# Two-block transformer layer in fp32, one core: how attention probabilities are normalised and turned

## Chip, cores and metric

The kernel runs on one NeuronCore of a Trainium2 chip. Everything is fp32. The metric is the device time of one execution in microseconds (us).

## What is computed

Two blocks in a row on 256 tokens of width 1024. The first block is an adaptive-norm layer with a mixer of two attentions and a mixture of 32 experts; the second has a gated linear recurrence, an LRU and a dense feed-forward part. The change touches only the softmax of the two attentions of the first block. Both have 8 heads of width 64; one selects keys and adds a distance bias, the other adds a forgetting bias. What follows the logits is the same in both:

```python
    logits = jnp.where(causal[None, None], logits, -jnp.inf)
    p = jax.nn.softmax(logits, axis=-1).astype(v.dtype)
    o = jnp.einsum('bhqs,bshd->bqhd', p, v)
```

## The kernel before, in words

**Layout.** Activations lie transposed (features on partitions, `L` = 256 tokens in the free dimension). All weights pass through `ring`, four slots filled by SyncE's DMA queue. The eight PSUM banks are `ps[:, 0..7, :]`. Each engine has one program written out by hand, and semaphores tie them.

**Attention.** The 16 heads go in 8 pairs, p = 0 to 7 (0 to 3 the forgetting heads, 4 to 7 the selecting ones), two "halves" per pair. Queries lie on partitions in two blocks of 128: block 0 sees keys 0 to 127 (columns 0 to 127 of `logit` and `prob`), block 1 sees all 256 keys (columns 128 to 383), so that a half is 128 x 384. For each pair:

1. TensorE, `logits_of(p)` (L821, L826): the dot products, into banks 2 and 3.
2. VectorE, `logits(p)` (L1860 to L1874): bias and mask into `logit`, then the negated row maximum.
3. ScalarE, `softmax(p)` (L1470, L1472): exp into `prob`, row sums into `p_sum`. From pair 1 on it waits until the same half of the pair before has been turned (`pt_done`), as `prob` has one buffer per half.
4. VectorE, `diagonals(p)` (L1882, L1887): reciprocal of the sums, and for each of the two query blocks `diag` = identity times that reciprocal, 128 x 128.
5. TensorE, `turn_probs(p)` (L837): for each half three products `prob_block.T @ diag`, which turn a 128 x 128 block and scale it at once, into bank 4 or 5. It waits for `diag_ready`, and for `pt_taken` of the pair before.
6. ScalarE, `turned_probs(p)` (L1481): copies the bank to `probT`.
7. TensorE, `values(p)` (L849), and ScalarE, `mixed(p)` (L1487, L1488): the head outputs.

**What lies between.** On TensorE the steps of a pair are spread among other work. For pairs 0 to 4 the order is `turn_probs(p)`, `logits_of(p+1)`, a 16-record group of `features` (L730, input projection), `values(p)`, `ada_rows` (L689, the modulation rows), another `features`, `ada_cols` (L700), `turn_probs(p+1)`. Pair 5 has `features` around it; pairs 6 and 7 have pieces of the output projection, `out_b` (L919), around them. Then come `out_a` (L929) mixed with `route_part` (L977, L979 and plain transposes of `hT` on L985), the routing chain on VectorE, the gather product (L1017), the experts (L1028, L1036 and L1039 transposes, L1049, L1056), and the second block.

**VectorE between the pairs.** After `diagonals(p)` it waits for `ada_cols`, adds a bias (L1794) and does four k-tiles of the modulation product (`ada_steps`, L1765, L1768); only then comes `logits(p+1)`. After pair 5 it makes a reciprocal (L1906) and scales four tiles (L1909).

**DMA.** SyncE issues each load when an event of TensorE has freed its slot: modulation and input weights (L434, L440, L444) and the first four experts (L485, L490) during attention and output projection, and from the expert loop on, gate/up and down weights by pairs of experts, first at 250.1 us.

Of the kernel before, what the change touches and what calls it, by code (L numbers as in the profile page):

```python
# [23 lines left out]
ALU = mybir.AluOpType  # L24
# [4 lines left out]
P = 128  # L29
L = 256  # L30
BLK = L // P
# [97 lines left out]
def build(nc, x, c, w_ada, b_ada, g_mix, w_in, b_forget, g_out_a, g_out_b, w_out, g_ffn, w_group,  # L129
# [3 lines left out]
    with ExitStack() as ctx:  # L133
        def sb(name, shape, dt=F32):
            return ctx.enter_context(nc.sbuf_tensor(name, shape, dt))

        def sem(name):
            return ctx.enter_context(nc.semaphore(name))
# [8 lines left out]
        ident = sb("ident", [P, P])  # L147
# [14 lines left out]
        def cut(at, *shape):  # L162

            n = 1
            for s in shape:
                n *= s
            v = arena[:, at:at + n]
            if len(shape) == 2:
                v = v.rearrange("p (a b) -> p a b", b=shape[1])
            if len(shape) == 3:  # L170
                v = v.rearrange("p (a b c) -> p a b c", b=shape[1], c=shape[2])
            return v
# [20 lines left out]
        logit = cut(8192, 2, NK)  # L193
        prob = cut(8960, 2, NK)
        probT = cut(9728, 2, NK)
        diag = cut(10496, 2, BLK, P)
        causal = cut(11008, L)
        neg_dist = cut(11264, NK)
        head_row = cut(11648, HEADS, P)
# [8 lines left out]
        p_rsum = att_small[:, 80:112].rearrange("p (n b) -> p n b", b=BLK)  # L208
# [63 lines left out]
        def state(ch):  # L272

            return tokf[:, (ch - 1) * 512:ch * 512] if ch <= 4 else sqf[:, (ch - 5) * 512:(ch - 4) * 512]
# [51 lines left out]
        ps = ctx.enter_context(nc.psum_tensor("ps", [P, 8, 512], F32))  # L326
# [26 lines left out]
        forget_abs, forget_ln, log_f_ready = sem("forget_abs"), sem("forget_ln"), sem("log_f_ready")  # L353
        cum_done, cum_taken = sem("cum_done"), sem("cum_taken")
        logits_done, logits_taken, logits_ready = sem("logits_done"), sem("logits_taken"), sem("logits_ready")
        probs_ready, diag_ready = sem("probs_ready"), sem("diag_ready")
        pt_done, pt_taken, pv_done, pv_taken = sem("pt_done"), sem("pt_taken"), sem("pv_done"), sem("pv_taken")
        mix_ready = sem("mix_ready")
        mo_done, mo_taken = sem("mo_done"), sem("mo_taken")
# [252 lines left out]
        def _(pe):  # L612
# [19 lines left out]
            for q in range(4):  # L632
                for k in (2 * q, 2 * q + 1):
                    for b in range(BLK):
                        at = (k % 2) * L + b * P
                        last = pe.transpose(ps[:, q, at:at + P], tok[:, b, k * P:(k + 1) * P], ident[:])
# [33 lines left out]
            for i in range(8):  # L670
                last = pe.matmul(ps[:, 0, i:16:8], lhsT=row0[:, i // 4, (i % 4) * P:(i % 4 + 1) * P], rhs=both_halves,
                                 start=True, stop=True)
# [92 lines left out]
            for b in range(BLK):  # L765
                last = pe.transpose(ps[:, 6, 8 * b:8 * b + 8], kI[64:72, b * P:(b + 1) * P], ident[64:72, 64:72])
# [29 lines left out]
            for q in (slice(0, HEADS), slice(64, 64 + HEADS)):  # L796
                pe.matmul(ps[q, 6, 128:384], lhsT=lf[:, 0, :], rhs=tri[:], start=True, stop=False)
                last = pe.matmul(ps[q, 6, 256:384], lhsT=lf[:, 1, :], rhs=tri[:, 0:P], start=False, stop=True)
# [31 lines left out]
            def turn_probs(p):  # L830

                for half in range(2):
                    pe.wait_ge(diag_ready, 2 * p + half + 1)
                    if p:
                        pe.wait_ge(pt_taken, 2 * p - 1 + half)
                    for s in range(3):
                        last = pe.matmul(ps[:, 4 + half, s * P:(s + 1) * P], lhsT=prob[:, half, s * P:(s + 1) * P],  # L837
                                         rhs=diag[:, half, min(s, 1), :], start=True, stop=True)
                    last.then_inc(pt_done, 1)

            def values(p):
# [17 lines left out]
            features(2, P)  # L859
            ada_cols(1)  # L860
            turn_probs(0)
            pe.wait_ge(tile_taken, 13)
            logits_of(1)
# [37 lines left out]
            for k in range(4, KT):  # L901
                last = pe.matmul(ps[:, 7, 0:L], lhsT=ones[:], rhs=sq[:, k, :], start=k == 4, stop=k == KT - 1)
# [64 lines left out]
            for k in range(4):  # L967
                pe.wait_ge(pv_taken, 2 * k + 10)
                last = pe.matmul(ps[:, 7, 0:L], lhsT=ones[:], rhs=sq[:, k, :], start=k == 0, stop=k == 3)
# [30 lines left out]
            for b in range(BLK):  # L1000
                last = pe.transpose(ps[:, 5, b * 65:b * 65 + 65], raw_rows[0:65, b * P:(b + 1) * P], ident[0:65, 0:65])
# [10 lines left out]
            for b in range(BLK):  # L1012
                pe.wait_ge(pick_ready, b + 1)
                for j in range(KT):
                    if j == KT - 1:
                        pe.wait_ge(pick_ready, BLK)
                    last = pe.matmul(ps[:, j, :], lhsT=tok[:, b, j * P:(j + 1) * P], rhs=pick[:, b, :],  # L1017
                                     start=b == 0, stop=b == BLK - 1)
# [90 lines left out]
            with pe.Else():  # L1109
                clear_banks()  # L1110
                with pe.Fori(0, EXPERTS // SLOTS) as i:
                    for u in range(2):
                        e0 = 2 * u
                        with pe.Fori(0, WINDOWS) as w:
                            n = i * (2 * WINDOWS) + w + u * WINDOWS
# [38 lines left out]
            for i in range(4):  # L1154
                o = bank2()
                for k in range(KT):
                    if i == 0:
                        pe.wait_ge(raw_ready, k + 1)
                    last = pe.matmul(o[:, 0:L], lhsT=w[:, k, i * P:(i + 1) * P], rhs=h_raw[:, k, :], start=k == 0,  # L1159
                                     stop=k == KT - 1)  # L1160
# [19 lines left out]
            for g in range(2):  # L1180
                for j in range(4):
                    last = pe.matmul(ps[:, 4 + 2 * g + j // 2, (j % 2) * L:(j % 2 + 1) * L],
                                     lhsT=gate_w[:, g, j, :], rhs=xc[:, j, :], start=True, stop=True)
# [12 lines left out]
            for b in range(BLK):  # L1196
                for h in range(HG):
                    last = pe.transpose(ps[:, 4 + b, h * P:(h + 1) * P], ks[:, h, b * P:(b + 1) * P], ident[:])
# [3 lines left out]
            for b in range(BLK):  # L1202
                t = slice(b * P, (b + 1) * P)
                for h in range(HG):
                    last = pe.matmul(ps[:, 6 + b, h * P:(h + 1) * P], lhsT=kd[:, h, t], rhs=raw_q[:, h, t],
                                     start=True, stop=True)
# [31 lines left out]
            for h in range(HG):  # L1238
                n = slice(h * P, (h + 1) * P)
                o = ps[:, 4 + h // 2, (h % 2) * L:(h % 2 + 1) * L]  # L1240
                for b in range(BLK):
                    pe.matmul(o[:, b * P:(b + 1) * P], lhsT=v_[:, b, n], rhs=sc_[:, b, h, :],
                              start=h % 2 == 0 and b == 0, stop=False, skip_group_check=True)
                for ch in range(1, CHUNKS):
                    t = slice(ch * CHUNK, (ch + 1) * CHUNK)
                    last = pe.matmul(o[:, t], lhsT=state(ch)[:, n], rhs=raw_q[:, h, t], start=False,
                                     stop=ch == CHUNKS - 1, skip_group_check=True)
# [22 lines left out]
            for t in range(FT):  # L1270
                ch, i = divmod(t, FFN_STEP)
                n = min(FFN_STEP, FT - ch * FFN_STEP)
# [7 lines left out]
                for half in range(2):  # L1280
                    at = (half * n + i) * P
                    for k in range(KT):
                        if t == 0 and half == 0:
                            pe.wait_ge(scaled[4], k + 1)
                        last = pe.matmul(ps[:, t % 4, half * L:(half + 1) * L], lhsT=w[:, k, at:at + P],  # L1285
                                         rhs=hT[:, k, :], start=k == 0, stop=k == KT - 1)
# [11 lines left out]
            def down_product(t, j, last=False):  # L1298

                ch, i = divmod(t, DOWN_STEP)  # L1300
                w = weights("down", ch, min(DOWN_STEP, FT - ch * DOWN_STEP), D)
                return pe.matmul(ps[:, 4 + j // 2, (j % 2) * L:(j % 2 + 1) * L], lhsT=w[:, i, j * P:(j + 1) * P],  # L1302
                                 rhs=ffn[:, t, :], start=t == 0 and j % 2 == 0, stop=t == FT - 1, skip_group_check=True)
# [13 lines left out]
            for t in range(first_late):  # L1317
# [3 lines left out]
                for j in range(KT):  # L1321
                    last = down_product(t, j)
# [4 lines left out]
            for i in range(4):  # L1327
                for t in range(first_late, FT):
                    for j in (2 * i, 2 * i + 1):
                        last = down_product(t, j)  # L1330
# [372 lines left out]
        def _(ve):  # L1703
            step = Count()

            def own(k=1):

                ve.wait_ge(dve_step, step.up(k))
# [50 lines left out]
            def ada_steps(c):  # L1759

                w, part = weights("ada", c, KT, ada_width(c)), ada_part(c)
                ve.wait_ge(arrived[SLOT["ada", c]], ARRIVED["ada", c])
                if c >= 2:
                    ve.wait_ge(ada_rows_done, c)
                ve.tensor_scalar(part, w[:, 0, :], silu_c[:, 0:1], None, ALU.mult).then_inc(dve_step, 1)  # L1765
                for k in range(1, DVE_K):
                    own()
                    ve.scalar_tensor_tensor(part, w[:, k, :], silu_c[:, k:k + 1], part, ALU.mult, ALU.add  # L1768
                                            ).then_inc(ada_part_ready if k == DVE_K - 1 else dve_step, 1)
# [33 lines left out]
            keys = (slice(0, P), slice(P, NK))  # L1803
# [70 lines left out]
                        ve.tensor_reduce(neg_max[:, n, b:b + 1], logit[:, half, keys[b]], AX.X, ALU.max, negate=True  # L1874
                                         ).then_inc(logits_ready, 1)

            def diagonals(p):

                for half in range(2):
                    n = 2 * p + half  # L1880
                    ve.wait_ge(probs_ready, n + 1)
                    ve.reciprocal(p_rsum[:, n, :], p_sum[:, n, :]).then_inc(dve_step, 1)  # L1882
                    own()
                    if p:
                        ve.wait_ge(pt_done, n - 1)
                    for b in range(BLK):
                        i = ve.tensor_scalar(diag[:, half, b, :], ident[:], p_rsum[:, n, b:b + 1], None, ALU.mult)  # L1887
                    i.then_inc(diag_ready, 1)

            for p in range(5):  # L1890
                logits(p)
                diagonals(p)
                add_bias(p + 1) if p < 4 else None
                if p < 4:
                    ada_steps(p + 2)
# [5 lines left out]
                             ).then_inc(dve_step, 1)  # L1901
            own(2)
            logits(5)
            diagonals(5)
            ve.wait_ge(std_ready, STD["b"])
            ve.reciprocal(rstd[:, 1, :], rstd[:, 1, :]).then_inc(dve_step, 1)  # L1906
            own()
# [1 line left out]
                ve.scalar_tensor_tensor(mixT[:, k, :], mixT[:, k, :], parB[:, k:k + 1], rstd[:, 1, :],  # L1909
                                        ALU.mult, ALU.mult).then_inc(mix_ready, 1)  # L1910
            logits(6)
            diagonals(6)
            logits(7)
            diagonals(7)


            lb0, lb1, lru = par(parB, PB_ROWS, "lb0"), par(parB, PB_ROWS, "lb1"), par(parB, PB_ROWS, "lru_a")
# [186 lines left out]
            with ve.Else():  # L2104
                with ve.Fori(0, EXPERTS // 2) as i:
                    with ve.Fori(0, WINDOWS) as w:
                        n = i * WINDOWS + w
# [118 lines left out]
            for ch in range(CHUNKS - 1):  # L2226
# [5 lines left out]
                for h in range(HG):  # L2232
                    n = slice(h * P, (h + 1) * P)
                    last = ch * CHUNK + CHUNK - 1
                    i = ve.scalar_tensor_tensor(state(ch + 1)[:, n], state(ch)[:, n], eb[:, h, last:last + 1],
                                                ps[:, 4 + ch % 4, n], ALU.mult, ALU.add)
# [86 lines left out]
```

## Time and profile before

| what | value |
|---|---|
| median of 3 runs | 872.6 us (872.42, 872.6, 874.89) |
| the profiled execution | 875.01 us |
| its span, first to last instruction | 873.3 us |
| mean granted TensorE clock | 0.985 |
| attention with its turns | about 86 to 190 us |
| output projection and routing | 190 to 224 us |
| gather and experts | 224 to 480 us |
| second block | 480 to 873 us |

How to read it: PE is TensorE's matmuls, PEld its weight loads, DVE VectorE, ACT ScalarE, SPq SyncE's DMA queue. An fp32 product of the program appears as two records (L837 has 96 for 48 products), a transpose as one (L985 has 16 for 16). A record's duration reaches past the start of the next, so that the rate is read from distances between starts, not from durations.

### The profile page before, as it was taken

Reading aid. Unit: us, or ns where it says so; the run is one execution under the profiler, and the core shown is the slowest. Engines: PE = TensorE matmul, PEld = TensorE weight load, DVE = VectorE, ACT = ScalarE, POOL = GpSimd, SP = SyncE. Lnnn points to the kernel's source line nnn. Section 1 sums busy time; section 2 is a strip of 40 time slices with the busy share of each in tenths; the row PEclk is TensorE's granted clock in tenths of the full one; section 3 lists DMA queues with packets and bytes.
Section 4 is the critical chain, followed back from the end, with each engine's and each line's share of the span. In section 5 each row is a group of like instructions: output and inputs, shape, how many; then the busy total and the mean of one; then the engine's idle time right before and its main releaser. Section 6 shows DMA issues by size and latency. Waiting matters only on the chain.

```text
span 873.3 us, 10154 instructions
## 1 busy us (share of the span) xinstructions
PE 829.3 (95%) x4067; PEld 592.2 (68%) x4067; DVE 264.5 (30%) x650; ACT 171.7 (20%) x360; POOL 14.4 (2%) x37
## 2 busy tenths in 40 slices
PE   4999999998789999999999889999999999999997
PEld 3578777786335454444444776788888888888886
DVE  4138546554412121212111576344111111110003
ACT  4123323433301010101101328122210000000001
POOL 2100000000010000000000000000000000000000
PEclk9999999999799999999999999998999999999999
DMA  9988665426159999999999922224434442444001
GB/s 374 374 230 302 235 247 199 167 123 244 46 211 418 418 417 420 414 420 416 419 417 318 338 97 97 70 77 143 152 137 145 145 144 53 160 168 199 0 1 49
DMA packets 67037, 196.58 MB, mean 225 GB/s; under 512 B 2767, under 2 KB 30776, under 8 KB 57784
## 3 DMA queue, kind: packets, MB, share of 16 engines
q1 hardware_dynamic: 66192, 195.37, 58.9%
q0 software_dynamic: 288, 0.41, 0.2%
q8 instruction: 27, 0.44, 0.2%
q10 hardware_dynamic: 520, 0.28, 0.1%
q14 instruction: 10, 0.08, 0.0%
HBM read 194.80 MB, written 1.05 MB: 224 GB/s over the span
## 4 chain that ended last, share of the span: by engine, by line
PE 83%; DMA 11%; DVE 2%; ACT 1%; issue 1%; SPq 0%; DVEq 0%
PE ps L1285 17%; DMA ring<-in_w_down 10%; PE ps L1302 9%; PE ps L1028 8%; PE ps L626 8%; PE ps L730 7%; PE ps L1049 4%; PE ps L1056 4%; PE ps L957 3%; PE ps L739 2%; PE ps L689 2%; PE ps L1017 2%; PE ps L919 2%; PE ps L929 2%; PE ps L1159 1%; PE ps L837 1%
## 5 line engine op out<-in xcount | busy, mean ns | idle before, releaser
L1285 PE MATMUL ps<-hT,ring 128*128 128x256 f32 x704 | 152.3, 379 | 0.9 <-DVE xT L2264 0.9
L1285 PEld LDWEIGHTS ps<-hT,ring 128*128 128x128 f32 x704 | 133.7, 190 | 19.4 <-issue 1.3
L1028 PE MATMUL ps<-ring,arena 128*64 128x512 f32 x512 | 113.2, 594 | 5.4 <-DMA ring<-in_w_down 3.1
L1028 PEld LDWEIGHTS ps<-ring,arena 128*64 128x64 f32 x512 | 38.8, 137 | 79.0 <-issue 73.0
L1302 PE MATMUL ps<-arena,ring 128*128 128x256 f32 x352 | 76.7, 380 | 0.3 <-PE ps L1285 0.3
L1302 PEld LDWEIGHTS ps<-arena,ring 128*128 128x128 f32 x352 | 66.6, 190 | 9.6 <-issue 0.7
L730 PE MATMUL ps<-hT,ring 128*128 128x256 f32 (+1 forms) x288 | 67.5, 390 | 1.2 <-ACT hT L1397 1.2
L730 PEld LDWEIGHTS ps<-hT,ring 128*128 128x128 f32 (+1 forms) x288 | 53.5, 190 | 13.9 <-issue 6.2
L1056 PE MATMUL ps<-arena 128*128 128x256 f32 x256 | 62.0, 386 | 0.9 <-DVE arena L2074 0.9
L1049 PE MATMUL ps<-ring,arena 128*64 128x512 f32 x256 | 58.5, 599 | 0.7 <-ACT arena L1575 0.7
L1056 PEld LDWEIGHTS ps<-arena 128*128 128x128 f32 x256 | 46.1, 190 | 18.9 <-issue 12.2
L626 PE MATMUL ps<-hT,ring 128*128 128x256 f32 x256 | 56.6, 380 | 2.4 <-DVE arena L2144 2.1
L626 PEld LDWEIGHTS ps<-hT,ring 128*128 128x128 f32 x256 | 48.2, 190 | 9.7 <-DVE hT L2139 2.5
L2275 DVE TENSOR_TENSOR arena<-ps,rstd 128x256 f32<-128x256 f32 x22 | 9.3, 424 | 120.4 <-PE ps L1285 120.3
L2071 DVE TENSOR_TENSOR arena<-arena,ps 128x256 f32<-128x256 f32 x16 | 6.7, 421 | 113.5 <-ACT arena L1573 113.5
L1049 PEld LDWEIGHTS ps<-ring,arena 128*64 128x64 f32 x256 | 17.0, 136 | 33.3 <-issue 32.4
L1687 ACT ACTIVATE arena<-arena 128x256 f32<-128x256 f32 x22 | 9.2, 416 | 135.1 <-DVE arena L2275 135.1
L2074 DVE COPY arena<-ps 128x512 f32<-128x512 f32 x16 | 11.1, 692 | 81.0 <-PE ps L1049 81.0
L957 PE MATMUL ps<-mixT,ring 128*128 128x256 f32 x128 | 28.6, 383 | 0.1
L957 PEld LDWEIGHTS ps<-mixT,ring 128*128 128x128 f32 x128 | 24.7, 193 | 5.3 <-issue 2.0
L1573 ACT ACTIVATE arena<-ps 128x256 f32<-128x256 f32 x16 | 6.2, 384 | 110.6 <-PE ps L1028 110.6
L2286 DVE TENSOR_TENSOR xT<-ps,xT 128x512 f32<-128x512 f32 x4 | 2.8, 691 | 73.6 <-PE ps L1302 73.6
(381 smaller groups left out, 848.4 us busy)
## 6 DMA issues: line engine op xcount, KB each, us to landing
ring<-in_w_gate SPq DMA_DIRECT2D x32, 1024.0 KB, 10.2
ring<-in_w_up SPq DMA_DIRECT2D x32, 1024.0 KB, 12.2
ring<-in_w_down SPq DMA_DIRECT2D x32, 1024.0 KB, 12.7
ring<-in_w_gate_up SPq DMA_DIRECT2D x14, 1536.0 KB, 9.4
ring<-in_w_ada SPq DMA_DIRECT2D x5, 3072.0 KB, 11.9
ring<-in_w_ada SPq DMA_DIRECT2D x9, 1024.0 KB, 13.0
ring<-in_w_in SPq DMA_DIRECT2D x9, 1024.0 KB, 15.8
ring<-in_w_down SPq DMA_DIRECT2D x3, 3072.0 KB, 10.2
```

What stands on the lines that cost most here:

```text
L626: last = pe.matmul(o, lhsT=w_of(k), rhs=rhs_of(k), start=k == 0, stop=k == k_n - 1)
L689: last = pe.matmul(ps[64 * half:64 * half + 64, 7, 0:n], lhsT=silu_b[:, k, :] if k < KT else ones[:, 0:64], rhs=w[:, k, cols] if k < KT el ...
L730: last = pe.matmul(o[0:n, 0:L], lhsT=w[:, k, lo:lo + n], rhs=hT[:, k, :], start=k == 0, stop=k == KT - 1)
L739: last = pe.matmul(o[:, i * n:(i + 1) * n], lhsT=hT[:, k, b * P:(b + 1) * P], rhs=w[:, k, lo:lo + n], start=k == 0, stop=k == KT - 1 and f ...
L919: last = pe.matmul(ps[:, m // 2, (m % 2) * L:(m % 2 + 1) * L], lhsT=w[:, k, (m % 4) * P:(m % 4 + 1) * P], rhs=mixT[:, k, :], start=m % 2 = ...
L929: last = pe.matmul(ps[:, 4 + m // 2, (m % 2) * L:(m % 2 + 1) * L], lhsT=w[:, k, (m % 4) * P:(m % 4 + 1) * P], rhs=mixT[:, k, :], start=m % ...
L957: last = pe.matmul(o, lhsT=w[:, k, (m % 4) * P:(m % 4 + 1) * P], rhs=mixT[:, k, :], start=last_of is None and m % 2 == 0 and k % 4 == 0, s ...
L1028: last = pe.matmul(ps[WIN * h:WIN * (h + 1), 0, :].rearrange("p (g n) -> p g n", g=2), lhsT=xw[:, u, k, WIN * h:WIN * (h + 1)], rhs=gu_w[: ...
L1049: last = pe.matmul(ps[WIN * h:WIN * (h + 1), 2 + half, :], lhsT=turned[:, u, at:at + WIN], rhs=dn[:, k, half * 512:(half + 1) * 512], star ...
L1056: last = pe.matmul(ps[:, 4 + j // 2, (j % 2) * L:(j % 2 + 1) * L], lhsT=y_sb[:, j * P:(j + 1) * P], rhs=turned[:, u, FE:FE + L], start=Fal ...
L1285: last = pe.matmul(ps[:, t % 4, half * L:(half + 1) * L], lhsT=w[:, k, at:at + P], rhs=hT[:, k, :], start=k == 0, stop=k == KT - 1)
L1302: return pe.matmul(ps[:, 4 + j // 2, (j % 2) * L:(j % 2 + 1) * L], lhsT=w[:, i, j * P:(j + 1) * P], rhs=ffn[:, t, :], start=t == 0 and j % ...
```

## The change

Instead of scaling an identity matrix and multiplying by it, VectorE scales `prob` in place, 128 columns for query block 0 and 256 for block 1, and TensorE turns each 128 x 128 block with its transpose against the constant identity. The tile `diag` goes, the semaphore is renamed, and VectorE's wait on `pt_done` ahead of writing `diag` goes.

```diff
@@ turn_probs (TensorE)
                 for half in range(2):
-                    pe.wait_ge(diag_ready, 2 * p + half + 1)
+                    pe.wait_ge(scaled_probs, 2 * p + half + 1)
                     if p:
                         pe.wait_ge(pt_taken, 2 * p - 1 + half)
                     for s in range(3):
-                        last = pe.matmul(ps[:, 4 + half, s * P:(s + 1) * P], lhsT=prob[:, half, s * P:(s + 1) * P],
-                                         rhs=diag[:, half, min(s, 1), :], start=True, stop=True)
+                        last = pe.transpose(ps[:, 4 + half, s * P:(s + 1) * P], prob[:, half, s * P:(s + 1) * P], ident[:])
                     last.then_inc(pt_done, 1)
@@ VectorE
-            def diagonals(p):
+            def scale_probs(p):
 
                 for half in range(2):
                     n = 2 * p + half
                     ve.wait_ge(probs_ready, n + 1)
                     ve.reciprocal(p_rsum[:, n, :], p_sum[:, n, :]).then_inc(dve_step, 1)
                     own()
-                    if p:
-                        ve.wait_ge(pt_done, n - 1)
                     for b in range(BLK):
-                        i = ve.tensor_scalar(diag[:, half, b, :], ident[:], p_rsum[:, n, b:b + 1], None, ALU.mult)
-                    i.then_inc(diag_ready, 1)
+                        i = ve.tensor_scalar(prob[:, half, keys[b]], prob[:, half, keys[b]], p_rsum[:, n, b:b + 1], None,
+                                             ALU.mult)
+                    i.then_inc(scaled_probs, 1)
```

All eight calls of `diagonals(p)` become `scale_probs(p)` at the same places.

## Rows read from the trace of the kernel before

**Rows 1.** The page: busy time by engine, and the chain that ended last.

```profile
PE 829.3 (95%) x4067; PEld 592.2 (68%) x4067; DVE 264.5 (30%) x650; ACT 171.7 (20%) x360; POOL 14.4 (2%) x37
...
PE 83%; DMA 11%; DVE 2%; ACT 1%; issue 1%; SPq 0%; DVEq 0%
```

**Rows 2.** Busy time by stretch: us, PE, PEld, DVE, ACT, POOL busy, clock, DMA share, GB/s.

```profile
98.00:190.00 92.00, 90.91 (x606) 71.96 (x605) 50.99 (x147) 34.71 (x107) 0.00 (x0) 1.00 0.59 224
190.00:220.00 30.00, 25.02 (x135) 19.52 (x133) 12.80 (x42) 11.20 (x20) 0.74 (x4) 0.97 0.55 201
```

**Rows 3.** Chain of waits in order of time: start us, us, what; the turns' pieces.

```profile
98.78 1.44 PE ps L837 x12
...
159.25 0.57 DVE arena L1860
...
165.50 0.39 ACT arena L1409
...
183.29 1.54 PE ps L837 x12
...
202.38 0.59 PE ps L985 x4
```

**Rows 4.** PE's timeline, two windows on pair 0's turn: start us, us, what.

```profile
98.64 1.58 PE L837 MATMUL ps<-arena 128*128 128x128 f32 x12
...
99.06 1.06 PE L837 MATMUL ps<-arena 128*128 128x128 f32 x8
```

**Rows 5.** PE's timeline, two windows on one group of transposes of `hT`.

```profile
202.31 0.66 PE L985 MATMUL ps<-ident,hT 128*128 128x128 f32 x4
...
202.48 0.49 PE L985 MATMUL ps<-ident,hT 128*128 128x128 f32 x3
```

**Rows 6.** Groups by line and shape, DVE, 84 to 190 us: busy us, mean ns.

```profile
L1887 DVE TENSOR_SCALAR arena<-ident,arena 128x128 f32<-128x128 f32 x32 | 7.7, 283 | 0.6
...
L1909 DVE SCALAR_TENSOR_TENSOR mixT<-mixT,parB,rstd 128x256 f32<-128x256 f32 x4 | 1.7, 481 | 0.0
...
L1765 DVE TENSOR_SCALAR tok<-ring,silu_c 128x256 f32<-128x256 f32 x1 | 0.4, 352 | 0.0
```

**Rows 7.** Timelines of DVE, ACT and PE around the turns of pairs 1, 5, 6, 7.

```profile
106.67 0.48 DVE L1887 TENSOR_SCALAR arena<-ident,arena 128x128 f32<-128x128 f32 x2
...
113.49 1.58 PE L837 MATMUL ps<-arena 128*128 128x128 f32 x12
...
164.14 0.48 DVE L1887 TENSOR_SCALAR arena<-ident,arena 128x128 f32<-128x128 f32 x2
...
166.79 1.60 PE L837 MATMUL ps<-arena 128*128 128x128 f32 x12
...
175.68 0.48 DVE L1887 TENSOR_SCALAR arena<-ident,arena 128x128 f32<-128x128 f32 x2
...
177.54 1.50 PE L837 MATMUL ps<-arena 128*128 128x128 f32 x12
...
180.63 0.84 ACT L1481 ACTIVATE arena<-ps 128x384 f32<-128x384 f32 x2
...
180.96 0.48 DVE L1887 TENSOR_SCALAR arena<-ident,arena 128x128 f32<-128x128 f32 x2
...
182.42 0.87 PE L849 MATMUL ps<-arena 128*64 128x256 f32 x8
...
183.22 1.60 PE L837 MATMUL ps<-arena 128*128 128x128 f32 x12
```

**Rows 8.** SyncE's queue, first expert loads of the loop; chain at the DMA-bound stage.

```profile
250.14 0.35 SPq L485 DMA_DIRECT2D ring<-in_w_gate x1
...
300.06 14.07 DMA ring<-in_w_down
```

**Rows 9.** Busy time by stretch, a fall of the clock and the 4 us behind it.

```profile
488.00:492.00 4.00, 4.00 (x12) 3.21 (x12) 3.82 (x7) 0.77 (x1) 0.00 (x0) 0.57 1.08 354
492.00:496.00 4.00, 4.00 (x21) 3.51 (x20) 0.83 (x2) 0.00 (x0) 0.00 (x0) 1.00 1.09 362
```

**Rows 10.** Single lines: transposes early and late in the trace, duration ns min/median/max.

```profile
L646 PE MATMUL ps<-ident,mixT x16: 421/421/448, 16.2 to 19.4; 128*128 128x128 f32 x16
...
L985 PE MATMUL ps<-ident,hT x16: 272/273/332, 202.3 to 215.7; 128*128 128x128 f32 x16
```

More of the change, by code:

```diff
@@ L195, in build @@
         probT = cut(9728, 2, NK)
-        diag = cut(10496, 2, BLK, P)
         causal = cut(11008, L)
@@ L355, in build @@
         logits_done, logits_taken, logits_ready = sem("logits_done"), sem("logits_taken"), sem("logits_ready")
-        probs_ready, diag_ready = sem("probs_ready"), sem("diag_ready")
+        probs_ready, scaled_probs = sem("probs_ready"), sem("scaled_probs")
         pt_done, pt_taken, pv_done, pv_taken = sem("pt_done"), sem("pt_taken"), sem("pv_done"), sem("pv_taken")
@@ L1883, in diagonals @@
                     own()
-                    if p:
-                        ve.wait_ge(pt_done, n - 1)
                     for b in range(BLK):
-                        i = ve.tensor_scalar(diag[:, half, b, :], ident[:], p_rsum[:, n, b:b + 1], None, ALU.mult)
-                    i.then_inc(diag_ready, 1)
+                        i = ve.tensor_scalar(prob[:, half, keys[b]], prob[:, half, keys[b]], p_rsum[:, n, b:b + 1], None,
+                                             ALU.mult)
+                    i.then_inc(scaled_probs, 1)
             for p in range(5):
                 logits(p)
-                diagonals(p)
+                scale_probs(p)
                 add_bias(p + 1) if p < 4 else None
@@ L1903, in _ @@
             logits(5)
-            diagonals(5)
+            scale_probs(5)
             ve.wait_ge(std_ready, STD["b"])
@@ L1911, in _ @@
             logits(6)
-            diagonals(6)
+            scale_probs(6)
             logits(7)
-            diagonals(7)
+            scale_probs(7)
             lb0, lb1, lru = par(parB, PB_ROWS, "lb0"), par(parB, PB_ROWS, "lb1"), par(parB, PB_ROWS, "lru_a")
```

## The prediction

> **What bounds the kernel.** I began with the page: TensorE is busy 95% of the span and the chain that ended last runs over it for 83% [rows 1]. What counts is the stretch with the turns, so next the busy time by stretch: from 98 to 190 us TensorE is busy 90.9 of 92 us, at granted clock 1.00, while VectorE has 51.0 and ScalarE 34.7 [rows 2]. All eight turns are there. Then the chain in order of time: every turn lies on it as one TensorE piece, 1.44 us for pair 0 and 1.54 for pair 7 [rows 3], and the six between are 1.34 to 1.53, 11.8 us in sum. The only stretch between turns where TensorE is not the bound begins at the end of pair 5's logits, 159.2 us: VectorE and ScalarE carry the chain until ScalarE's copy at 165.5 us [rows 3]. It starts from a TensorE event, so that it moves with it. TensorE time taken out of a turn is thus time taken out of the chain, as long as nothing else is late.
>
> **TensorE, the term that counts.** Before, a turn is six products, 12 records. In the middle of a turn 8 records span 1.06 us, the last of them 0.275 long, so (1.06 - 0.275)/7 = 0.112 us lie between starts [rows 4]; a product is two records, 0.224 us. After, the turn is six transposes. The trace has the very operation, 128 x 128 fp32 against the identity, at full clock: three on L985 span 0.49 us with a last one of 0.273, so (0.49 - 0.273)/2 = 0.109 us lie between starts [rows 5, 10]. A transpose takes one record where a product takes two, at nearly the same spacing. 8 pairs x 6 = 48, and 48 x (0.224 - 0.109) = 5.5 us. That is the upper bound. For the lower bound I take whole pieces of the chain with their heads: four transposes on L985 are 0.59 us there, 0.148 each [rows 3], so six are 0.885 and eight turns 7.1 us against 11.8: 4.7 us. Part of those 0.59 us is the first distance (0.17 us from 202.31 to 202.48 [rows 5]), paid once per group, and a turn has such a head before as well: it runs 1.58 us from 98.64, where 11 even distances and a last record would be 1.51 [rows 4]. I am therefore near the upper end and take 5.4 us.
>
> A rule that speaks against this. The L985 records are 273 ns long [rows 10], yet start 0.109 us apart. The Trainium skill, "TensorE: Matmul & The Clock Gate", Part 4 (PE-mode transpose), gives about 275 ns for a 128x128 transpose inside a kernel. The trace agrees as to a record's length and not as to the rate; read as a cost paid one after another, the page's figure would make 48 x 0.275 = 13.2 us of the turns, 1.4 us more than now.
>
> **VectorE.** Per half, two 128-column multiplications (0.48 us as a pair [rows 7], 283 ns each [rows 6]) become one of 128 and one of 256 columns. A 256-column tensor_scalar from and to SBUF takes 352 ns [rows 6]: 0.07 us more per half, 1.1 us in all. In place is not shown for this form; the nearest row is L1909, which writes where it reads with a third operand, 481 ns [rows 6]. That is the upper bound: 0.2 us per half, 3.2 in all; the lower is 0. I take 0.07, as the form with one tensor operand is the nearer. It costs nothing as long as the scaled half is there when TensorE asks:
> - Pairs 0 to 4: VectorE finishes pair 1 at 107.15 us and the turn starts at 113.49 [rows 7]; 6.3 us of cover. The other four of this form stand alike.
> - Pair 5: done at 164.62, turned at 166.79 [rows 7]. 2.2 us, fixed by the chain between, since both follow the same ScalarE copy or lie ahead of it.
> - Pair 6: done at 176.16, turned at 177.54 [rows 7]. 1.4 us; the second half alone decides, and it needs 0.07 to 0.2.
> - Pair 7: done at 181.44; turned at 183.22 [rows 7], now 0.7 us sooner, since pair 6's turn lies between. 1.1 us of cover, less twice 0.07.
>
> **What is late next.** `values(6)` at 182.42 us would come at 181.74. It needs ScalarE's two copies, which end at 181.47 [rows 7] and sit behind exp of pair 7, itself behind VectorE's maxima, themselves behind pair 6's scaling: 0.07 us later. 181.5 plus a semaphore step against 181.7: it just fits; with the slow in-place price it would wait some 0.1 us. I book 0.1 us in the 5.4. The exp of the next pair waits for the turn of the one before, which comes sooner. VectorE's dropped wait on `pt_done` is worth nothing: the exp it follows has waited for the same turn. `diag` takes no DMA; no queue, load or issue is moved.
>
> **Does the gain reach the end?** The loads of attention are released by TensorE events, and a pair's loop shrinks by 0.7 us at a time, with loads landing microseconds ahead (DMA share only 0.59 there [rows 2]). The experts are bound by DMA from 300 us (a piece of 14.07 us on the chain [rows 8]), but their loop's first issue, at 250.14 us [rows 8], is itself released by TensorE's work; the stream starts sooner by the same 5.4 us. So nothing swallows it.
>
> **Sum.** Against the profiled execution: 875.01 - 5.4 = 869.6 us, a span of 873.3 - 5.4 = 867.9. That execution was 2.4 us above the median of 872.6, one of the three runs (874.89) lies with it and two at 872.4 to 872.6. By the median: 872.6 - 5.4 = 867.2 us. No change that a measurement here can tell is within 0.3%, 2.6 us.
>
> **Rivals.**
> 1. *Half the gain is given back by the cover of the late pairs.* If a scaled half comes 1 us later than reckoned at pairs 6 and 7, TensorE waits there. Against it: 0.07 to 0.2 us are added where over 1 us is free. To matter each of four instructions must take 0.5 us more; then 1 to 2 us go, and the time is 868.2 to 869.2, still faster. If the turns also have only the lower bound's 4.7 us, 870 or just above: within 0.3%. 9%.
> 2. *The clock, ending slower.* Granted clock is 1.00 through all turns [rows 2]. Place: the 14 us periods with the turns. Were the clock to fall to its lower level once a turn, each fall would cost what the one at 488 us costs: 12 matmul records in 4 us, against 21 in the next 4 [rows 9], 9/21 x 4 = 1.7 us. Eight are 13.7 us: 872.6 - 5.4 + 13.7 = 880.9 us. It decides from the fourth fall on (3 x 1.7 = 5.1 is still paid by the gain; to be slower by over 0.3% takes five). For it: the transposes on L646 took 421 ns each where the later ones took 273 [rows 10], so 16 in a row from 16.2 to 19.4 us ran at the slow pace. Against it: those on L985 came in groups of four from 202 to 216 us at full pace, among products as here, and a turn is now only 0.7 us between dense products. 4%. The same page and part of the Trainium skill say that the clock gate does not count transposes as activity; by that rule the L646 row is as expected, and the turns would be 0.7 us holes, which this trace does not show to matter.
> 3. *It does not do what it says:* the turns' time is set by something other than the number of records, such as the stationary tile's load, and a transpose next to attention data costs as a product: no gain, 872.6. Against it: L985 has the same shape, types and roles, 0.109 apart [rows 5]. 3%.
> 4. *The clock's falls elsewhere move* as everything after 190 us comes sooner: the fall at 488 us and its like may be 1.7 us shorter or longer, and the runs' spread of 2.5 us is of this size. This shifts the result both ways and is in the range, not a case.
>
> My forecast, gain 4.7 to 5.5 us to the end, has 84%.
>
> **Range.** Low: 872.6 - 5.5 - 1.7 = 865.4, rounded to 865.2. High: 872.6 - 4.7 + 2.3 (most of the spread, which also takes in rival 1) = 870.2. Chances: faster by over 0.3% (below 870.0) 0.87, of the forecast and the better part of rival 1; same 0.09; slower 0.04.
>
> **What would show it.** Right: L837's successor has 48 records 0.11 us apart and pieces of about 0.75 to 0.85 us on the chain; VectorE's scaling about 350 ns on 256 columns; the expert loop's first issue near 244.8 us; the gather and the second block as long as before. Wrong: a wait of the turn or of `values` on VectorE or ScalarE (rival 1), a granted clock under 1.00 between 98 and 185 us (rival 2), transposes 0.22 us apart (rival 3), or a first expert issue that is sooner by 5 us and a span that is not.

## The result, and the profile after

The changed kernel takes 863.31 us (median of 4, 861.58 to 863.81), the kernel before, run beside it, 873.75 us (4, 872.42 to 875.79). The ratio is 0.9874, 95% interval 0.9845 to 0.9904: faster by 11.0 us, between 8.4 and 13.5. The forecast was a gain of 5.4 us and 867.2 us; the measured time lies below its range of 865.2 to 870.2 us.

The turns behave as forecast. The chain in order of time of the changed kernel, its pieces at the turns and at the transposes of `hT` (L836 is the line that was L837):

```profile
98.37 0.71 PE ps L836 x6
112.48 0.72 PE ps L836 x6
127.39 0.81 PE ps L836 x6
...
153.51 0.71 PE ps L836 x6
...
172.91 0.66 PE ps L836 x6
...
196.18 0.59 PE ps L983 x4
```

Six records each, 0.66 to 0.81 us, where the kernel before has twelve in 1.34 to 1.54 (two of them in [rows 3]); the eight pieces sum to 6.03 us against 11.82. VectorE's scaling by shape, in the groups of the same stretch:

```profile
L1883 DVE TENSOR_SCALAR arena<-arena 128x256 f32<-128x256 f32 x16 | 5.6, 348 | 0.0
L1883 DVE TENSOR_SCALAR arena<-arena 128x128 f32<-128x128 f32 x16 | 4.6, 287 | 0.6
```

348 ns in place on 256 columns, as L1765 in [rows 6] (352), not as L1909. And the tightest place, pairs 6 and 7, in the timeline:

```profile
170.89 0.55 DVE L1883 TENSOR_SCALAR arena<-arena 128x128 f32<-128x128 f32 x2
...
172.75 0.82 PE L836 MATMUL ps<-ident,arena 128*128 128x128 f32 x6
...
175.91 0.85 ACT L1479 ACTIVATE arena<-ps 128x384 f32<-128x384 f32 x2
...
176.24 0.55 DVE L1883 TENSOR_SCALAR arena<-arena 128x128 f32<-128x128 f32 x2
...
176.95 0.87 PE L847 MATMUL ps<-arena 128*64 128x256 f32 x8
...
177.75 0.88 PE L836 MATMUL ps<-ident,arena 128*128 128x128 f32 x6
```

Pair 6 is scaled by 171.44 us and turned from 172.75; `values(6)` starts at 176.95, 0.2 us behind the copies' end at 176.76; pair 7 is scaled by 176.79 and turned from 177.75. `values(6)` starts 4.20 us behind its turn's start, against 4.88 before ([rows 7]): the 0.68 us are the shorter turn, so nothing was lost to a wait. Only the releaser is new: the 0.33 us that TensorE's weight load sits idle there now end with ScalarE's copy, where before the same third of a microsecond was "issue".

**Where the rest came from.** The two profiled executions differ by 13.4 us. Matmul starts on four marks divide it: A is the first product of the gather, B the first of the last expert pair's 32 gate and up records, C the product of `ones` with `sum_gsq` in the stage behind the expert loop, D the last matmul.

| stretch | before | after | gained |
|---|---|---|---|
| up to pair 0's turn | 98.64 | 98.23 | 0.4 |
| turn 0 to A | 125.83 | 119.54 | 6.3 |
| A to B (gather, experts) | 240.30 | 240.16 | 0.1 |
| B to C (leaving the expert loop) | 34.46 | 31.16 | 3.3 |
| C to D (second block) | 368.18 | 364.88 | 3.3 |

Of the 6.3 us, 5.8 are the turns, and 0.5 are the ranking products ahead of the gather, which took 1.51 us at the lower clock before and 0.99 now. The last two rows, 6.6 us, lie more than 250 us behind the change. Look at the chain at B to C, before and then after:

```profile
475.95 3.61 PE ps L1049 x16
...
482.08 3.50 ACT tok L1590 x8
485.58 1.53 issue
487.11 12.29 PE ps L1159 x48
499.39 0.45 PE ps L1165 x2
```

```profile
469.11 3.61 PE ps L1047 x16
...
475.24 3.51 ACT tok L1588 x8
478.75 1.18 issue
479.92 9.33 PE ps L1157 x42
489.26 0.45 PE ps L1163 x2
```

"issue" is waiting that no instruction of the profile explains. Before, all 48 records of the first products behind the loop come after it; after, only 42 do: PE's timeline has the other six earlier.

```profile
477.11 1.46 PE L1157 MATMUL ps<-tok,ring 128*128 128x256 f32 x6
479.92 9.33 PE L1157 MATMUL ps<-tok,ring 128*128 128x256 f32 x42 [1.36 <-issue]
```

Queue 8 carries instructions. Between its loads at 641.1 and 668.0 us of the kernel before TensorE has 126 matmuls and 126 weight loads:

```profile
641.10:668.00 26.90, 26.90 (x126) 23.67 (x126) 5.77 (x12) 3.14 (x6) 0.00 (x0) 1.00 0.35 118
```

252 records and a few waits per load of 16,384 bytes; over the nine stretches between loads from 610 to 858 us it is 245 to 275 instructions, 257 in the mean. So the queue loads TensorE's program, 64 bytes an instruction, 256 to a piece, and each record is an instruction. (The Trainium skill, "Runtime: NRT & Kernel Launch", Terms, has each engine's instruction memory refilled in blocks of 16 KiB; the trace agrees.) A product is four instructions and a transpose two, so the change makes TensorE's program 48 x 2 = 96 instructions shorter. (The code behind the expert loop stands behind an `Else` branch that is not taken here, so TensorE also jumps there.) The DMA queues from just after B to the time when the code behind the loop is wanted, before (464.7 to 484.0 us) and after (457.9 to 477.1 us):

```profile
q1 hardware_dynamic: 4346, 6.67, 100.0%
q14 instruction: 2, 0.02, 0.2%
```

```profile
q1 hardware_dynamic: 4312, 6.61, 99.1%
q8 instruction: 1, 0.02, 0.3%
q14 instruction: 2, 0.02, 0.2%
```

After, a piece of TensorE's code is loaded during the last expert pair (at 460.6 us); before, none is until the loop has been left (484.4 us). The end of such a load is what TensorE waits for: before, its packets end at 485.5 us and the 48 records start at 487.1; after, those of the next piece run from 477.4 to 478.4 us, and the 42 records start at 479.9, 1.6 and 1.5 us behind them. C to D has another cause, the granted clock. Before, then after, around the same products:

```profile
592.00:602.00 10.00, 10.00 (x49) 8.70 (x49) 0.40 (x1) 4.33 (x6) 0.00 (x0) 0.66 0.68 244
```

```profile
582.00:592.00 10.00, 10.00 (x61) 8.55 (x61) 2.57 (x1) 4.92 (x7) 0.00 (x0) 1.00 0.67 241
```

The clock was at its lower level (1.2 instead of 2.4 GHz) from 593.9 to 600.7 us before, and not at all here after.

### The profile page after: what moved, and what is told of

Its sections match the earlier page's. It is cut to its first block, busy times and chain, and to the rows that moved or that the text cites. A ratio compares the mean times of both kernels' runs of the same rounds, so it can differ in the third digit from the quotient of the medians.

```text
span 859.9 us, 10044 instructions
## 1 busy us (share of the span) xinstructions
PE 817.5 (95%) x4019; PEld 581.6 (68%) x4019; DVE 265.7 (31%) x650; ACT 170.7 (20%) x360; POOL 14.3 (2%) x37
## 4 chain that ended last, share of the span: by engine, by line
PE 83%; DMA 11%; DVE 3%; ACT 1%; issue 1%; SPq 0%; DVEq 0%
PE ps L1283 18%; DMA ring<-in_w_down 10%; PE ps L1300 9%; PE ps L1026 8%; PE ps L625 8%; PE ps L729 7%; PE ps L1047 4%; PE ps L1054 4%; PE ps L955 3%; PE ps L738 2%; PE ps L688 2%; PE ps L1015 2%; PE ps L917 2%; PE ps L927 2%; DMA ring<-in_w_ada 1%; PE ps L651 1%
## 5 line engine op out<-in xcount | busy, mean ns | idle before, releaser
L1283 PEld LDWEIGHTS ps<-hT,ring 128*128 128x128 f32 x704 | 133.7, 190 | 19.4 <-issue 1.3
L729 PEld LDWEIGHTS ps<-hT,ring 128*128 128x128 f32 (+1 forms) x288 | 53.5, 190 | 13.8 <-issue 6.1
L1054 PEld LDWEIGHTS ps<-arena 128*128 128x128 f32 x256 | 46.1, 190 | 18.9 <-issue 12.2
## 6 DMA issues: line engine op xcount, KB each, us to landing
ring<-in_w_up SPq DMA_DIRECT2D x32, 1024.0 KB, 12.2
ring<-in_w_in SPq DMA_DIRECT2D x9, 1024.0 KB, 15.2
```

The source lines that it names most:

```text
L729: last = pe.matmul(o[0:n, 0:L], lhsT=w[:, k, lo:lo + n], rhs=hT[:, k, :], start=k == 0, stop=k == KT - 1)
L1054: last = pe.matmul(ps[:, 4 + j // 2, (j % 2) * L:(j % 2 + 1) * L], lhsT=y_sb[:, j * P:(j + 1) * P], rhs=turned[:, u, FE:FE + L], start=Fal ...
```

## The experiments

**Theories.** A: the gain is TensorE's. A1: what goes beyond the turns comes from the later stages starting sooner; A2: from transposes in place of products, whenever the stages start. B: VectorE's in-place scaling has a share. C: the place of TensorE's code against the 16 KB pieces has a share. D (last run only): small work in an idle stretch keeps the clock up.

### One half of the change at a time

e1_pe_only: the kernel before, `diag` still written but not used; the probabilities stay undivided by their sum.

```diff
-  last = pe.matmul(ps[...], lhsT=prob[...], rhs=diag[:, half, min(s, 1), :], start=True, stop=True)
+  last = pe.transpose(ps[...], prob[...], ident[:])
```

> VectorE still writes the scaled identity into diag, TensorE turns prob with plain transposes (so the probabilities stay unscaled: the division by the row sum is left out). Theory A (the whole gain is TensorE's, at the turns and in what follows from coming sooner): as the changed kernel, 863.3 +- 1.5 us. Theory B (scaling in place on VectorE has a share in it): between 865 and 870 us.

Measured: 862.25 us (861.63 to 862.91), ratio to before 0.9866 (0.9833 to 0.9899).

e2_dve_only: the changed kernel with products by the identity.

```diff
-  last = pe.transpose(ps[...], prob[...], ident[:])
+  last = pe.matmul(ps[...], lhsT=prob[...], rhs=ident[:], start=True, stop=True)
```

> VectorE scales prob in place, TensorE still multiplies, now by the constant identity. Theory A: as the kernel before, 873.7 +- 1.5 us, with 96 records at the turns, 0.112 us apart. Theory B: 868 to 871 us.

Measured: 874.37 us, ratio 1.0001 (0.9978 to 1.0024), and 96 records again:

```profile
L836 PE MATMUL ps<-ident,arena x96: 273/275/377, 99.3 to 185.2; 128*128 128x128 f32 x96
```

B falls: the whole gain comes with TensorE's transposes (which shorten both the turns and the code), and VectorE's scaling costs and gives nothing that the interval of 2 us lets one see.

### The time or the kind of the work

e3_twice issues every transpose two times:

```diff
-  for s in range(3):
+  for s in (0, 1, 2, 0, 1, 2):
```

> The changed kernel with each transpose issued twice into the same place (12 records a turn again). Theory A1 (the 4 to 5 us that the turns do not show come from everything after 190 us starting 5.8 us sooner, which shifts it against the clock's falls and the loads): time back to that of before, 873.7 +- 1.5 us. Theory A2 (those 4 to 5 us come from the transposes replacing products, whenever the later stages start): 863.3 + 5.8 = 869 us.

Measured: 874.65 us, ratio 0.9987 (0.9966 to 1.0008). Its turns are pieces of 1.31 to 1.46 us, 11.3 in sum.

e4_pad48 adds work that nobody uses at the end of attention:

```diff
   pe.wait_ge(pt_taken, 16)
+  for _ in range(48):
+      pe.transpose(ps[:, 4, 0:P], ident[:], ident[:])
```

> The changed kernel with 48 more transposes of the identity into a free PSUM bank at the end of attention, ahead of the output projection's second half (48 x 0.109 = 5.2 us of TensorE). Theory A1: the later stages start where they did before, so 872 to 874 us, with the clock's falls near 488 and 594 us back in the record. Theory A2: 863.3 + 5.2 = 868.5 us, without those falls.

Measured: 874.78 us, ratio 0.9998 (0.9981 to 1.0016), with a fall of the clock from 488.3 to 491.7 us and none near 594.

A2 falls: with twelve transposes a turn, or the same work elsewhere, all 11 us are gone, though only some 5.2 us of work came back. This looked like A1. But both edits also make the program 96 instructions longer, exactly as long as it was. That confounds A1 with a theory that I had not had: C.

### Start time against length of the code

The next kernels tear the two apart. Instructions that do nothing go in where TensorE idles; they move all the code behind them. First with satisfied waits (two to an instruction), 96 ahead of the load of `x`, more in the next gap:

```diff
   pe.wait_ge(ident_ready, 1)
+  for _ in range(192):
+      pe.wait_ge(ident_ready, 1)
   pe.wait_ge(x_there, 16)
```

> The changed kernel with 96 more instructions in TensorE's program, waits that are already satisfied, put where TensorE idles for the load of x: its code has the length of the one before, its work and its times at the turns stay. Theory C (a part of the gain comes from the code being 96 instructions shorter, which moves it against the 16 KB pieces in which queue 8 loads TensorE's code): the gather still starts near 218 us, but the first product behind the expert loop comes 2 to 3 us later relative to it, and the time is 866 to 869 us. Theory A1 (only coming sooner counts): 863.3 +- 1.5 us.

> The kernel before with 160 more such instructions (96 ahead of the load of x, 64 in the next idle stretch): its code stands against the 16 KB pieces (256 instructions) as that of the changed kernel does, its turns are the slow ones. Theory C: 863.3 + 5.8 = 869 us, +- 1.5. Theory A1: as the kernel before, 873.7 to 875.4 us.

> The changed kernel with 160 such instructions. Theory C: the piece of code behind the expert loop is loaded in time wholly, the 1.4 us wait 6 records into the product behind the loop goes, 861 to 862.5 us. Theory A1: 863.3 +- 1.5 us.

For e8, with waits in the two gaps and 16 instructions of them ahead of the ranking:

```diff
   pe.wait_ge(pt_taken, 16)
+  for _ in range(12):
+      pe.matmul(ps[:, 4, :], lhsT=ident[:], rhs=sqf[:, 1024:1536], start=True, stop=True)
```

> The changed kernel with 12 products of 512 columns at the end of attention (12 x 2 records x 0.213 = 5.1 us of TensorE, 48 instructions) and 208 satisfied waits, so that the later stages start as late as before while the code stands as that of the changed kernel. Theory C: 863.3 + 5.1 = 868.4 us, +- 1.5. Theory A1: 873.7 to 875.4 us.

Measured, medians: e5 868.45 (864.18 to 871.75), ratio 0.9927; e6 873.77 (871.18 to 879.9), 0.9997; e7 865.68 (865.04 to 866.42), 0.9887; e8 880.02 (879.2 to 882.95), 1.0061. e5 falls into the range of theory C; e6 and e7 came over 3 us above theirs, e6 even into that of A1, because a satisfied wait is not free (the first matmul came at 12.05 us in place of 5.88, and turn 0 at 101.25 to 101.68 us in place of 98.23 or 98.64). e8 came 11.6 us above its value, above A1's range as well, for two reasons: turn 0 at 105.51 us, and the twelve wide products, whose 24 records start 0.429 us apart, 10.3 us in all, where 0.213 had been booked. The stretches behind the gather, which don't contain that delay, are in the table below. So I repeated the three with a padding that ends inside the idle stretches, small transposes:

```diff
+  for _ in range(48):
+      pe.transpose(ps[:, 7, 256:264], ident[0:8, 0:P], ident[0:8, 0:8])
   for b in range(BLK):
       pe.wait_ge(xn_ready, b + 1)
```

(e10 and e11 have 32 more of them ahead of the wait for `x`.)

> The changed kernel with 48 transposes of an 8 x 128 corner of the identity (96 instructions, a weight load and a matmul each) put into TensorE's idle stretch from 11 to 16 us, so that its code has the length of the one before and no stage starts later. Theory C (place of the code against the pieces in which it is loaded): last matmul minus first gather product 639 to 643 us as in the kernel before, against 636.2 now; median 866 to 869 us. Theory A1 (only the starts of the stages count): 863.3 +- 1.5 us.

> The kernel before with 80 such small transposes (160 instructions: 32 pieces of work while x is loaded, 48 from 11 to 16 us), so that its code stands as that of the changed kernel. Theory C: last matmul minus first gather product 636.3 us, median 863.3 + 5.8 = 869 us. Theory A1: as the kernel before, 873.7 to 875.4 us.

> The changed kernel with the same 160 instructions. Theory C: the wait of 1.4 us inside the first product behind the expert loop goes and nothing else moves, 861.5 to 863 us, which would be the fastest of all. Theory A1: 863.3 +- 1.5 us.

Measured: e9 867.62 (865.64 to 870.96), ratio 0.9924 (0.9901 to 0.9948); e10 872.39 (868.71 to 874.75), 0.9972 (0.9953 to 0.9992); e11 863.96 (862.34 to 868.19), 0.9893 (0.9864 to 0.9921). e9 lies in theory C's range, e10 between the two theories' (869 and 873.7 us and more), e11 above C's and within A1's. Turn 0 still came 0.9 to 2.0 us late, in e9 and e11 in part by a longer stretch at the lower clock near 35 us. With that delay the medians fit C: e9 should be 1.9 + 3.1 = 5.0 us slower than the changed kernel and is 4.3, e10 should be 3.1 - 0.9 = 2.2 us faster than the kernel before and is 2.4 (0.7 to 4.1). And from the first gather product to the last matmul, where theory C had forecast 639 to 643 us for e9 and 636.3 for e10, the profiles have 643.1 and 636.7.

All profiles, sorted by the length of TensorE's code against the changed kernel's (modulo 256 instructions, one piece). "Load" is the first load of queue 8 after B, in us after B; falls are stretches at the lower clock between the gather and D, in the profiled execution alone (each kernel has three or four more: ahead of 45 us, around the start of the gather, and behind D).

| kernel | code | records a turn | A | B to C | load | C to D | falls, us |
|---|---|---|---|---|---|---|---|
| before | +96 | 12 | 224.5 | 34.46 | 19.6 | 368.18 | 488 to 491, 594 to 601 |
| e2 | +96 | 12 | 225.1 | 34.20 | 19.4 | 364.88 | 244 to 248, 490 to 493 |
| e3 | +96 | 12 | 224.2 | 34.34 | 19.8 | 366.56 | 243 to 246, 488 to 492, 598 to 601 |
| e4 | +96 | 6 | 224.1 | 34.05 | 19.3 | 364.88 | 243 to 246, 488 to 492 |
| e5 | +96 | 6 | 221.3 | 34.55 | 19.7 | 364.89 | 485 to 488 |
| e9 | +96 | 6 | 220.1 | 34.24 | 19.4 | 368.18 | 484 to 487, 590 to 597 |
| after | 0 | 6 | 217.8 | 31.16 | 2.7 | 364.88 | none |
| e1 | 0 | 6 | 218.1 | 31.14 | 2.8 | 364.90 | none |
| e6 | 0 | 12 | 227.2 | 31.22 | 3.0 | 364.88 | none |
| e8 | 0 | 6 | 235.4 | 31.31 | 19.7 | 364.88 | none |
| e10 | 0 | 12 | 225.4 | 31.29 | 3.2 | 364.88 | none |
| e7 | +160 | 6 | 221.2 | 29.54 | 6.7 | 366.56 | 498 to 501 |
| e11 | +160 | 6 | 220.3 | 29.53 | 6.9 | 366.56 | 498 to 501 |
| e12 | +128 | 6 | 218.6 | 29.54 | 12.2 | 366.57 | 496 to 499 |

B to C falls into three groups that don't overlap, by the length of the code alone: 34.05 to 34.55, 31.14 to 31.31, 29.53 to 29.54 us. Turns of 6 and of 12 records lie in both of the first two, and starts of the gather from 217.8 to 235.4 us. A1 falls for this stretch; C is shown for it. In all eleven kernels of the first two groups the record behind the stop starts 1.3 to 1.6 us after the packets of a load of queue 8 have ended; in the three of the last group TensorE doesn't stop. (e8 had its piece loaded at 295.1 us already, inside the loop; its next load comes at 495.1 us, as the second one of the changed kernel does at 477.4.) No run separates the loop's end from the jump over the `Else` branch as what makes the load late. C to D is the clock alone: 364.9 us in the eight profiles without a fall there, 366.6 in the four with one of 3.4 us, 368.2 in the two with one of 6.8. The chain of e9, turns of 6 records and long code, is as that of the kernel before, with all 48 records behind the wait:

```profile
478.06 3.50 ACT tok L1590 x8
481.56 1.31 issue
482.87 12.29 PE ps L1159 x48
```

and that of e6, turns of 12 records and short code, is as that of the changed kernel:

```profile
484.76 3.51 ACT tok L1594 x8
488.27 1.24 issue
489.51 9.33 PE ps L1163 x42
```

In e11 the wait is gone altogether, and the 48 records take 10.36 us at full clock:

```profile
480.05 10.36 PE ps L1161 x48
490.41 0.45 PE ps L1167 x2
```

### A faster kernel?

e12_after_mid64 pads where the routing leaves TensorE idle (40 and 24 of the small transposes, 128 instructions), right ahead of the gather.

> The changed kernel with 64 small transposes (128 instructions) in the two stretches in which TensorE waits for the routing, 40 and 24 of them, ahead of the gather. Theory C: with 128 more instructions the piece of code behind the expert loop is loaded in time, from the last expert product to the last of the product behind the loop 26.7 us as in the kernels with 160 more, against 28.3; a code of another length would be needed to lose anything. Theory D (the clock falls ahead of the gather because TensorE stands idle for the routing, so small work there keeps it up): no fall at 214 us, first to last gather product 14.2 us or less against 15.2. If both hold, 860 to 861.5 us, faster than either kernel. If neither, 863.3 +- 1.5 us.

Measured: 862.51 us (861.43 to 866.67), ratio to before 0.9868 (0.9839 to 0.9898). C's part came as expected (B to C 29.54). D's did not: the clock was low from 215.7 to 222.5 us all the same, and the gather took 15.3 us against 15.2. (The Trainium skill, "TensorE: Matmul & The Clock Gate", Part 4, says that transposes don't count as activity for the clock; this run agrees, with its fall from 215.7 to 222.5 us, but transposes so small are a weak test of it.) And the 1.6 us won behind the loop were given back by a fall of the clock at 496 to 499 us, as in e7 and e11. No padding beats the changed kernel by more than the spread of its runs.

## Why the prediction was wrong

- **Turns.** Right in kind, slightly small: 5.8 us on the chain against 5.4 booked and 5.5 as "the upper bound". A piece before held 0.13 us more than 12 spacings (11.82/8 against 12 x 0.112), one after 0.10 more than six.
- **VectorE and the covers.** Right: 348 ns in place, no wait at pairs 5 to 7, `values(6)` 0.2 us behind the copies' end and not delayed. e2 shows that the scaling is worth nothing either way.
- **The gain reaches the end.** Right: A to B lost nothing of it; the expert loop's first issue came at 243.13 us, 7.0 us sooner than before.
- **The step that failed** is the end of "What is late next": "no queue, load or issue is moved". One was: TensorE's own program, 96 instructions shorter, and so the moment at which the code behind the expert loop is loaded. That is 3.1 us, a term that the prediction put at nothing (mean of B to C, 34.3 of six kernels against 31.2 of five). Some 1.9 us of the 3.3 between the two profiles are the clock (48 records in 12.29 us, against 10.36 in e11), the rest are the six records that no longer stand behind the wait. All six kernels of the long code have a fall at 484 to 490 us, none of the five of the short code does. So rival 4, which booked the clock's falls as a shift both ways, was wrong as well: this one goes with the long code and comes only with it.
- **Rivals 1 to 3** did not come: no fall of the clock in the turns, no late half, transposes 0.11 us apart.
- **The base** was low, too: the prediction counts from 872.6 us, the median of three runs, where the four groups of runs of the kernel before that stand beside the experiments have medians of 874.96 to 875.99 us.
- **The rest is time at the lower clock, and its cause is open.** 5.8 + 3.1 = 8.9 us, inside the interval of 8.4 to 13.5 us, but below its centre of 11.0; e1 has the same terms and is 11.7 us faster than before. Every run has its span and its mean granted clock c, and 2 x (1 - c) x span estimates its time at the lower level (26.2 us for the profiled execution before, whose falls sum to 26.8). The mean of that is 25.6 us over the 70 runs of the kernel before that stand beside the experiments, 17.2 over the four of the changed kernel and 13.8 over the four of e1, and among the 70 a microsecond more of it goes with 0.5 us more of span. So the changed kernel and e1 have 8 to 12 us less of it, by estimate 4 to 6 us of time (at most, as a part lies where TensorE idles), of which the fall behind the loop explains 1.7 to 1.9.
- **What brings the other falls** is not shown to be the length of the code: the estimate is 23.6 to 25.5 us for the five other kernels with the long code, but of the padded ones with the short code e8 has 15.1 us and e6 and e10 have 23.9 and 21.5. The "none" of the table holds for the profiled executions alone, and that of the changed kernel is its run with the highest clock (0.992, the others 0.988 to 0.990), which is also why the two profiles differ by 13.4 us and the medians by less. No run holds the clock fixed.

## What to carry to other kernels

For a 128 x 128 block, an fp32 transpose is one record where an fp32 product is two, at the same 0.11 us spacing: use it where a diagonal product only scales and turns, and let an idle engine scale. Any edit that changes the number of instructions moves all code behind it against the pieces in which it is loaded; where a loop or a skipped branch ends, look for "issue" on the chain and for the instruction queue's loads there, and before a surprise is put down to the edited stage, pad the other version to the same length. Measure stretches between marks as well as the whole: the stretch B to C varied by at most 0.5 us among kernels of one code length, where the runs of a single kernel spread over 1.3 to 8.7 us.

## What the runs showed of the hardware

- A piece of TensorE's code that is loaded late shows on the chain as 1.1 to 1.6 us of "issue" in the eleven kernels where TensorE stopped for one; it went on 1.3 to 1.6 us after the load's packets had ended. In the six with the long code it had stood idle for 2.6 to 3.1 us, and a fall of the clock began from 0.4 us ahead of its going on to 1.1 us behind; in the five with the short code, where six or seven records went ahead and the stop took 1.3 to 1.5 us, none did.
- Satisfied waits cost TensorE time: in e5, 96 instructions of two waits each start from 1.58 to 11.83 us, 0.11 us apart, and the first matmul comes at 12.05 us.
- A transpose of an 8 x 128 piece costs half of a whole one, though its data are a sixteenth: in e9, 48 of them run from 11.06 to 16.09 us, 0.107 us apart, and the sixteen 128 x 128 ones right behind start 0.217 us apart (16.27 to 19.53 us). The trace's clock records begin only at 19.7 us; the sixteen go at the pace of L646 in [rows 10], which is half that of L985.
- An fp32 record of 512 columns costs twice one of 256: 24 of them start 0.429 us apart in e8, those of 256 columns (L1157 of the changed kernel) 0.215.
